# Transposing and multiplying attention weights four heads at a time in a two-model kernel

## What is computed

```python
def fox_attention(q, k, v, log_f):
    ...
    def one_block(args):
        qi, ci, i = args
        s = jnp.einsum('bqhd,bkhd->bhqk', qi.astype(jnp.float32), kf) * scale
        s = s + ci[..., None] - c[:, :, None, :]
        ...
        s = jnp.where(mask[None, None], s, NEG_INF)
        p = jax.nn.softmax(s, axis=-1).astype(v.dtype)
        return jnp.einsum('bhqk,bkhd->bqhd', p, v)

def second_block(x, norm_g, fox_w_in, ...):
    for i in range(DEPTH):
        h = rmsnorm(x, norm_g[i])
        ...
        y = y * jax.nn.silu(gate)
        x = x + y @ w_out
    return rmsnorm(x, final_g)
```

## Time and profile before

| | us |
|---|---|
| median of 3 runs | 1783.79 (1783.46 to 1789.45) |
| profiled execution, time | 1782.65 |
| its span | 1780.9 |
| PE busy | 1762.0 (99%) |
| DVE busy | 1311.4 (74%) |
| ACT busy | 900.0 (51%) |
| mean of the 64 copies of 384 columns | 0.481 |
| their sum | 27.5 |

### The profile page before, as it was taken

The page is one execution under the profiler, slowest core; times in us unless marked ns, Lnnn a source line. Parts: engine busy times, 40 slices in busy tenths (PEclk is TensorE's granted clock), DMA queues, the critical chain, the costliest instruction groups (busy, mean ns, idle before and its releaser), DMA issues.

```text
span 1780.9 us, 35710 instructions
## 1 busy us (share of the span) xinstructions
PE 1762.0 (99%) x14365; PEld 1677.1 (94%) x14365; DVE 1311.4 (74%) x2088; ACT 900.0 (51%) x1326; POOL 40.1 (2%) x48
## 2 busy tenths in 40 slices
PE   8999999999999999999999999999999999999997
PEld 8999999999999999999999899998989999999876
DVE  7899899977679987998777765555565656666754
ACT  5433665545533456456565464545455443565553
POOL 0000000000000000000000110100100000000000
PEclk9999999999999999999999999999999999999999
DMA  7666655555666664556566666566655566545553
GB/s 232 189 207 190 190 143 175 191 190 194 196 186 207 192 200 142 155 191 199 180 201 185 203 184 202 181 201 182 195 165 165 191 190 174 155 146 162 161 190 130
DMA packets 199826, 325.54 MB, mean 183 GB/s; under 512 B 14783, under 2 KB 66191, under 8 KB 199565
## 3 DMA queue, kind: packets, MB, share of 16 engines
q1 hardware_dynamic: 197085, 320.85, 58.3%
q10 hardware_dynamic: 2608, 2.84, 0.5%
HBM read 320.42 MB, written 2.69 MB: 181 GB/s over the span
## 4 chain that ended last, share of the span: by engine, by line
PE 94%; DVE 5%; ACT 0%; issue 0%; DMA 0%; DVEq 0%; SPq 0%; ACTq 0%
PE g L495 73%; PE g L506 11%; PE att L641 2%; PE att L620 2%; PE att L596 2%; DVE w_lo L913 2%; DVE cacc L1159 2%; ACT w_hi L1534 0%; PE att L495 0%; PE att L793 0%; DMA stage<-in_w_in_dram 0%; PE att L850 0%; PE att L572 0%; PE att L873 0%; PE att L851 0%
## 5 line engine op out<-in xcount | busy, mean ns | idle before, releaser
L913 DVE TENSOR_TENSOR w_lo<-stage,w_hi 128x1024 fp32r<-128x1024 f32 x577 | 707.3, 1233 | 390.2 <-ACT w_hi L1534 389.3
L1534 ACT CAST w_hi<-stage 128x1024 fp32r<-128x1024 f32 x577 | 599.2, 1050 | 592.6 <-PE g L495 394.4
L495 PE MATMUL g<-a_hi,w_hi 128*128 128x256 f32 x2496 | 704.1, 282 | 2.5 <-DVE w_lo L913 1.6
L495 PE MATMUL g<-a_hi,w_lo 128*128 128x256 f32 x2496 | 693.6, 278 | 0.0
L495 PE MATMUL g<-a_lo,w_hi 128*128 128x256 f32 x2496 | 693.6, 278 | 0.0
L495 PEld LDWEIGHTS g<-a_hi,w_hi 128*128 128x128 f32 x2496 | 470.4, 188 | 12.8 <-issue 10.8
L495 PEld LDWEIGHTS g<-a_hi,w_lo 128*128 128x128 f32 x2496 | 470.3, 188 | 1.5 <-issue 1.2
L495 PEld LDWEIGHTS g<-a_lo,w_hi 128*128 128x128 f32 x2496 | 470.5, 188 | 0.0
L495 PE MATMUL g<-b_hi,w_hi 128*128 128x256 f32 x1440 | 403.1, 280 | 0.4 <-DVE w_lo L913 0.3
L495 PE MATMUL g<-b_hi,w_lo 128*128 128x256 f32 x1440 | 399.9, 278 | 0.0
L495 PE MATMUL g<-b_lo,w_hi 128*128 128x256 f32 x1440 | 399.9, 278 | 0.0
(11 more groups left out here) (231 smaller groups left out, 1378.3 us busy)
## 6 DMA issues: line engine op xcount, KB each, us to landing
stage<-in_fox_w_in_dram SPq DMA_DIRECT2D x128, 512.0 KB, 4.1
stage<-in_w_in_dram SPq DMA_DIRECT2D x112, 512.0 KB, 3.9
stage<-in_swa_w_in_dram SPq DMA_DIRECT2D x72, 512.0 KB, 3.8
stage<-in_w_in_dram SPq DMA_DIRECT2D x128, 256.0 KB, 3.1
stage<-in_w_out_dram SPq DMA_DIRECT2D x64, 512.0 KB, 4.3
stage<-in_w_pg_dram SPq DMA_DIRECT2D x64, 512.0 KB, 4.1
stage<-in_fox_w_out_dram SPq DMA_DIRECT2D x32, 512.0 KB, 4.6
stage<-in_swa_w_out_dram SPq DMA_DIRECT2D x32, 512.0 KB, 4.3
```

Source lines behind the costliest of these rows:

```text
L495: mm = pe.matmul(acc[:, j * S:(j + 1) * S], w[:, slot, c0 + j * P:c0 + (j + 1) * P], xx[:, k, :], start=st and m == 0 and j % 2 == 0, stop ...
L913: dve.tensor_tensor(w_lo[:, slot, :], stage[:, slot, :], w_hi[:, slot, :].bitcast(F32), ALU.subtract).then_inc(*t.inc("w_split"))
L1534: act.copy(w_hi[:, slot, :], stage[:, slot, :]).then_inc(*t.inc("w_rounded"))
```

## The change

For the causal groups (fox and swa) `heads4` takes the place of `heads`, with three interruptions at slots 7, 11 and 15. `turn4` transposes four heads, 12 tiles of 128 columns, side by side over three banks (TB, OB, MB seen as one, `TURNED4`). ACT copies them with two copies of 768 columns (`copy_four`) to `pt`, which grows from 2 x 512 to 3 x 512 columns. `attend4` multiplies the values of four heads and writes to SB (heads 0 to 3) or MB (heads 4 to 7). The gating reads SB in place of OB. ACT's copies stand at hooks 4 and 6 in place of 3, 4, 5 and 6.

```diff
-        pt = sb("pt", [2, 4 * P])
+        pt = sb("pt", [3, 4 * P])
...
+        TURNED4 = AA[:, CH:4 * CH]
+        pt4 = pt[:, :, :].rearrange("p a b -> p (a b)")
...
+            def turn4(lot):
+
+                def go():
+                    pe.wait_ge(*t.again("t_free"))
+                    pe.wait_ge(*t.see("normed", 4))
+                    if lot == 0:
+                        pe.wait_ge(*t.again("s_free"))
+                        pe.wait_ge(*t.again("ob_free"))
+                        pe.wait_ge(*t.again(misc_reader[0]))
+                    for n in range(4):
+                        j = 4 * lot + n
+                        for m, (kb, qb) in enumerate(tiles("causal")):
+                            c, _ = score_cols("causal", qb)
+                            at = (3 * n + m) * P
+                            mm = pe.transpose(TURNED4[:, at:at + P], uw[:, j, c + kb * P:c + (kb + 1) * P], ident[:, :])
+                    mm.then_inc(*t.inc("pt_done", 4))
+                    t.skip("t_free", 4)
+                return go
+
+            def attend4(lot, values):
+
+                def go():
+                    pe.wait_ge(*t.again("t_free"))
+                    dst = (SB, MB)[lot]
+                    for i in range(2):
+                        for kb in range(NB):
+                            first = kb
+                            for j in (4 * lot + 2 * i, 4 * lot + 2 * i + 1):
+                                c = (3 * (j % 4) + 2 * kb) * P
+                                mm = pe.matmul(dst[half(j):half(j) + HD, i * S + first * P:(i + 1) * S], values(j, kb),
+                                               pt4[:, c:c + (NB - first) * P], start=i == 0 and kb == 0, stop=kb == NB - 1,
+                                               skip_group_check=True)
+                    mm.then_inc(*t.inc("att_done", 4))
+                    if lot:
+                        t.skip("ob_free")
+                        t.skip("mb_free")
+                        misc_reader[0] = "mb_free"
+                return go
+
+            def heads4(values, slots, extra=()):
+                return {slots[0]: [turn4(0)], slots[1]: [*extra, attend4(0, values), turn4(1)], slots[2]: [attend4(1, values)]}
...
-                chunk("T", A, 1, work=heads("causal", fox_values, 7, [taken]))
+                chunk("T", A, 1, work=heads4(fox_values, (7, 11, 15), [taken]))
...
-                for lot, src in enumerate((OB, MB)):
+                for lot, src in enumerate((first, MB)):
...
+            def copy_four():
+
+                act.wait_ge(*t.see("pt_done", 4))
+                for n in range(2):
+                    act.copy(pt4[:, 6 * n * P:6 * (n + 1) * P], TURNED4[:, 6 * n * P:6 * (n + 1) * P]).then_inc(*t.inc("t_free", 2))
...
-                chunk({0: [exps("fox", (2, 3, 4, 5))], 1: [exps("fox", (6, 7))], 3: [copy_turned("fox", (0, 1))],
-                       4: [copy_turned("fox", (2, 3))], 5: [copy_turned("fox", (4, 5))], 6: [copy_turned("fox", (6, 7))]})
+                chunk({0: [exps("fox", (2, 3, 4, 5))], 1: [exps("fox", (6, 7))], 4: [copy_four], 6: [copy_four]})
```

More of the change, by code:

```diff
@@ L883, in _ @@
                 chunk("T", A, 0, work={4: [turn_q]} | swa_scores())
-                chunk("T", A, 1, work=heads("causal", swa_values, 7))
+                chunk("T", A, 1, work=heads4(swa_values, (7, 11, 15)))
             chunk("T", A, 0, work={4: [turn_q]} | swa_scores())
-            work = heads("causal", swa_values, 7)
+            work = heads4(swa_values, (7, 11, 15))
             chunk("N", B, 1, ready=True, order=EARLY, pieces=6, end=False, work=work)
@@ L1040, in norms, with gated @@
                 return go
-            def gated():
+            def gated(first=OB):
                 dve.wait_ge(*t.see("gate_act"))
                 dve.wait_ge(*t.own())
-                for lot, src in enumerate((OB, MB)):
+                for lot, src in enumerate((first, MB)):
                     dve.wait_ge(*t.see("att_done", 4))
@@ L1402, in fox_attention @@
                 chunk({0: [evac(1, scaled(gate[:, :, :]))],
-                       1: [gated, low_of(gate[:, :, :], B[0][:, part(g, CT), :], B[1][:, part(g, CT), :])]})
+                       1: [lambda: gated(SB), low_of(gate[:, :, :], B[0][:, part(g, CT), :], B[1][:, part(g, CT), :])]})
             with t.loop(dve, "fox", 3) as g:
@@ L1455, in _ @@
                 chunk({0: [evac(0, scaled(gate[:, :, :]))], 1: [norms("swa", 0)], 2: [norms("swa", 1)]})
-                gated()
+                gated(SB)
                 low_of(gate[:, :, :], B[0][:, bass.ds(g * CT, CT), :], B[1][:, bass.ds(g * CT, CT), :])()
@@ L1460, in _ @@
             chunk({0: [evac(0, scaled(gate[:, :, :]))], 1: [norms("swa", 0)], 2: [norms("swa", 1)],
-                   7: [gated, low_of(gate[:, :, :], B[0][:, 12:16, :], B[1][:, 12:16, :])]})
+                   7: [lambda: gated(SB), low_of(gate[:, :, :], B[0][:, 12:16, :], B[1][:, 12:16, :])]})
             def row_add(parity, c, blocks=range(NB), pieces=PIECES, event="gemm_done"):
@@ L1649, in _ @@
                 act.wait_ge(*t.again("att_done"))
-                fetch(pt[:, :, 0:S], p[l, 0].rearrange("(b s) d -> s b d", s=P), "p_in")
+                fetch(pt[:, 0:2, 0:S], p[l, 0].rearrange("(b s) d -> s b d", s=P), "p_in")
                 def glu_sig(n):
@@ L1809, in _ @@
                 chunk()
-                chunk({0: [exps("swa", (0, 1, 2, 3))], 1: [exps("swa", (4, 5, 6, 7))], 3: [copy_turned("swa", (0, 1))],
-                       4: [copy_turned("swa", (2, 3))], 5: [copy_turned("swa", (4, 5))], 6: [copy_turned("swa", (6, 7))],
+                chunk({0: [exps("swa", (0, 1, 2, 3))], 1: [exps("swa", (4, 5, 6, 7))], 4: [copy_four], 6: [copy_four],
                        7: [gate_silu(2)]})
@@ L1815, in _ @@
             chunk({0: [exps("swa", (0, 1, 2, 3))], 1: [exps("swa", (4, 5, 6, 7))],
-                   3: [copy_turned("swa", (0, 1))], 4: [copy_turned("swa", (2, 3))],
-                   5: [copy_turned("swa", (4, 5)), gate_silu(2)],
-                   6: [copy_turned("swa", (6, 7))], 7: [high_of(gate[:, :, :], B[0][:, 12:16, :], "mb_free")]})
+                   4: [copy_four], 5: [gate_silu(2)],
+                   6: [copy_four], 7: [high_of(gate[:, :, :], B[0][:, 12:16, :], "mb_free")]})
             def row_square(c):
```

## The result

The changed kernel takes 1792.55 us (median of 8 runs, 1788.97 to 1794.96) against 1785.09 us for the kernel before (8 runs, 1783.46 to 1790.59): ratio 1.0033, 95% interval 1.0022 to 1.0045. It is **0.3% slower** by the ratio; the medians differ by 7.5 us. It is outside the predicted range. The profiled execution took 1790.38 us; its span is 1788.6 against 1780.9.

What follows compares the result with a forecast made beforehand. The prediction took TensorE (PE), busy 99% of the span, as the bound. From the profiled 1782.65 us it took 4.8 for merging and added 1.4 for waits: 1779.3, stated as 1779 us, range 1774 to 1788.

Steps and rivals of the forecast that it cites:

- What bounds the kernel: Whole kernel: PE is busy 99% of the span, so only microseconds that PE does not need come off the end.
- Part 1, merging: Causal groups: two of five interruptions go, work unchanged; 5.90 us for 6.50 a group, 4.8 us saved for eight.
- The scores' 6.6: Other measure of merging, from score interruptions: 0.41 us each, 6.6 us for sixteen; its rival (1774 us) had 11%.
- Part 2, the wait for four heads: First turning waits for four normalised heads, not two: 0.2 us in seven groups, 1.4 us lost, range 0 to 2.6.
- Parts 3 to 5: ACT's fewer, larger copies; values in SB, transposes in TB, OB, MB; full groups keeping five interruptions: each costs nothing.
- The second effect: PE's two projection pitches, 0.1126 and 0.1171 us, in stretches within groups: no change, plus or minus 1.8 us.
- the slow pitch that stays on: Rival: third interruption leaves PE slow until the next interruption, 2,100 matmuls, 9.5 us more, 1788 to 1789 us; 14%.
- were followed by the fast pitch every time: Argument against the slow-pitch rival: value matmuls alone were followed by the fast pitch every time it can be read.
- is there an even number of times: Argument against the slow-pitch rival: two turnings, two values, so if each kind flips or leaves the pitch, groups end fast.
- only at an interruption: Claim about PE's projection stream: the pitch changes only at an interruption and then holds.
- The clock: Rival: longer transposes and narrow matmuls lower PE's clock; a piece per group at doubled distance, 19 us, 1798 us; 4%.
- The test named at the end: Sign in the profile after: matmuls between 1050 and 1095 us stay 0.113 us apart; 0.118 means the slow-pitch rival.

Runs made afterwards that it cites:

- split_last: Changed kernel with its last interruption taken apart into two of one pair of heads each, at slots 13 and 15: 1781.46 us, ratio 0.9984 to the kernel before.
- the second probe: Kernel before plus sixteen idle interruptions in fox's output projection, of other kinds than the first such run (1, 3, 24 transposes, mixtures, one-column matmuls): 1812.56 us, one execution.
- append2: Changed kernel with first turning at slot 8 and two idle transposes right behind the values of each group's last interruption: 1778.59 us, ratio 0.9955 to the kernel before.
- both probes: Two runs of the kernel before, each with sixteen idle interruptions (transposes, value-like matmuls) in fox's output projection, differing in kinds: 1807.69 and 1812.56 us.
- before_fox2: Kernel before with two idle transposes at slot 3 of the chunk behind each of the four fox groups: 1784.92 us, ratio 1.0006.
- before_fox4v: Kernel before with eight records of idle value matmuls (256 columns) at slot 3 of the chunk behind each fox group: 1797.10 us, ratio 1.0074.
- turn_first8: Changed kernel with first turning at slot 8 and the middle interruption's transposes put ahead of its values: 1789.67 us, ratio 1.0023 to the kernel before.

## Why the prediction was wrong

**What bounds the kernel** was right: PE at 99%, and every microsecond came from PE.

**Part 1, merging,** was right within 0.02 us: 1.33, 2.92 and 1.65 us were predicted, 1.35 (without the wait), 2.92 and 1.65 read. In all eight groups it took 4.8 us off without the waits, the 4.8 of the sum. The scores' 6.6 was not reached.

**Part 2, the wait for four heads,** was right in kind and half as large: 0.74 us against 1.4. 0.28 us in the first fox group, 0.22 and 0.23 in the second and third swa laps, none in the other fox laps, which PE now reached later, since it had gone slowly. In split_last, where it had not, PE waited in every fox lap, and with swa's laps 1.6 us in all. So the size was right for a kernel that keeps its pitch.

**Parts 3 to 5,** at nothing, were right in the price. A pair of ACT's copies takes 1.5 us, less than the 1.72 allowed, and ACT's waits ahead of them are fewer, but not longer, as was forecast: 0.60 and 1.92 us in the first fox group, where three of the four were 2.5 us or more. The second:

```profile
1046.78 1.51 ACT L1651 COPY pt<-att 128x768 f32<-128x768 f32 x2 [1.92 <-PE att L668]
```

PE's waits for `w_lo` did not grow (1.6 us before, 1.4 after, by line 498's first form):

```profile
L498 PE MATMUL g<-a_hi,w_hi 128*128 128x256 f32 x2496 | 706.0, 283 | 2.4 <-DVE w_lo L958 1.4
```

**The second effect is the step that failed.** It was "left at no change, with plus or minus 1.8 us", and measured +10.2 us. The rival beside it, the slow pitch that stays on, had the place (the end of the third interruption), the mechanism and nearly the price (9.5 us, 1788 to 1789; the profiled execution took 1790.4). It had 14% and should have had more; its own sum, 1779.3 + 9.5 = 1788.8 us, lay above the upper end of the stated range, 1788, which was said to take in most of it. I set against it that values alone "were followed by the fast pitch every time". That is true of the kernel before, 11 times of 11, and says nothing: every one of them was entered slow. The pitch ahead of it has to be read along with the pitch behind. The same trace held the other half, since scores are of the same width: of 20 such interruptions ten went from slow to fast and ten from fast to slow. One of each, windows behind the scores at 160.36 us and behind those that follow (65 and 67 matmuls in 7.4 us):

```profile
162.80:170.20 7.40, 7.40 (x65) 1.00 0.78 216
173.20:180.60 7.40, 7.40 (x67) 1.00 0.23 77
```

Read so, the attention's values turn the pitch over, and it matters whether the last ones are entered slow (before) or fast (after). The argument that each kind "is there an even number of times" was unsound in a second way: it treats an interruption as the sum of its kinds. The attention's values and six transposes turned the pitch over in 168 of 168 cases; its values and twelve never left it slow.

Nor does the pitch change "only at an interruption". In the kernel before it turns slow at 290.3 us, where the projection goes over to another operand (`pe_hi`) with nothing between: 12 steps of 0.113 us, then 18 of 0.119 us on average (timeline of PE, the ends of both):

```profile
288.83 0.28 PE L495 MATMUL g<-a_lo,w_hi 128*128 128x256 f32 x1
...
290.19 0.28 PE L495 MATMUL g<-a_lo,w_hi 128*128 128x256 f32 x1
290.31 0.28 PE L495 MATMUL g<-pe_hi,w_hi 128*128 128x256 f32 x1
...
292.45 0.28 PE L495 MATMUL g<-pe_hi,w_hi 128*128 128x256 f32 x1
```

At 712.6 us it goes from slow to fast among equal matmuls, at a single step of 0.149 us. In the long chunks behind the fox groups no such change shows ahead of the first matmuls of 512 columns or the end of the stage.

**The clock** did not fall: 1.00 in every window, also around 24 transposes in a row in the second probe, 2.63 us with no gap (timeline of PE, and a window of its matmuls):

```profile
1420.63 2.78 PE L608 MATMUL att<-ident 128*128 128x128 f32 x24
```

```profile
1420.00:1424.00 4.00, 4.00 (x38) 1.00 0.55 166
```

That column alone would be weak evidence, since it reads 1.00 in the earlier trace rows, too, from which this rival took its price of a doubled distance; but behind no interruption of the changed kernel's causal groups do the matmuls settle at more than 0.118 us. The Trainium skill, "TensorE: Matmul & The Clock Gate", Part 4 (PE-mode transpose), says that transposes do not count as busy in the way that matmuls do. In pieces as short as these it decided nothing.

**The test named at the end** of the prediction was the right one: "0.118 there is the slow-pitch rival". It was the first thing to look at, and it was so (367 matmuls in 43 us).

**What stays open.** What sets the pitch behind an interruption, since the same kinds gave both results at different places, and what the two pitches are. In the slow one PE's matmuls stand 0.118, 0.118, 0.117 us apart and in the fast one 0.113, 0.113, 0.114, at the same clock; no engine waits in either.

## What to carry to other kernels

When an engine is 99% busy with one repeated pair of instructions, measure the distance between two of them in every stretch, ahead of and behind each interruption, before counting interruptions: here 4% of pitch over 2,400 matmuls outweighed the 16 interruptions that were saved. To read what an event does to a state, tabulate the state ahead of it as well; a column that shows one outcome may only show one starting point. And if a merge leaves the stream in the worse of two pitches, a few cheap instructions right behind the last one may bring it back (append2: 0.23 us a group against 10 us in all), but only a trace tells whether they do at that place.

## What the runs showed of the hardware

- TensorE has two steady distances for this stream of weight loads and matmuls of 256 columns, 0.1133 and 0.1178 us, at a granted clock of 1.00 in both. The Trainium skill, "TensorE: Matmul & The Clock Gate", section "Back-to-back issue gap", gives 262 cycles for an isolated matmul of 256 columns, which at 2.4 GHz would be 0.109 us, by estimate; for a stream of weight loads and matmuls it has no figure at 256 columns. The traces show 0.113 or 0.118 us in such a stream, 4 or 8% more.
- A transpose of 128x128 inside the stream costs 0.11 to 0.12 us with no fixed part: one 0.117 us, two 0.23, twelve 1.32, twenty-four 2.63 (differences to the undisturbed pitch, both probes).
- The pitch also goes with the scatter of one kernel's executions (how much of it, the few traces don't show). In the first model two stretches of 1,066 and 1,018 matmuls (the last projections of its two layers, from 383 and 846 us) are fast in 13 and in 11 of the 16 traces and slow in the others, and each is worth about 4.7 us (1,066 or 1,018 x 0.0045). Windows of 100 us in them, in the kernel before and in before_fox2's profiled execution:

```profile
390.00:490.00 100.00, 100.00 (x885) 1.00 0.61 195
860.00:960.00 100.00, 100.00 (x884) 1.00 0.61 193
```

```profile
390.00:490.00 100.00, 100.00 (x851) 1.00 0.60 189
860.00:960.00 100.00, 100.00 (x851) 1.00 0.60 192
```

  That execution took 1793.32 us, where the median of its kernel is 1784.92. Of the kernels with several executions, five (append2, before_fox2, before_fox4v, split_last, turn_first8) have a trace with such a slow stretch, and each time it is one of the three slowest executions of its kernel. None of these five changes the work of the first model or its order, so the code alone does not decide it (what does, no run shows), and 2 us between two profiled executions prove nothing about an edit.
